# First chunk's rows of the delta rule loaded into other buffers beside the last projections, and the running sum's products issued one column block later

## What is computed

```
proj = x @ w_in                       # qkv, z, beta, a, and more
qkv  = silu(causal_conv(qkv, 4 taps))
q, k = l2norm(q) * 128**-0.5, l2norm(k);  v
beta = sigmoid(beta_logit);  g = -exp(a_log) * softplus(a + dt_bias)
G    = cumsum(g) in a chunk           # the running sum
decay = exp(G_i - G_j), lower triangle
L = strict lower((k*beta) k^T * decay);  T = (I + L)^-1
W = T (k*beta*exp(G));  U = T (v*beta);  A = (q k^T) * decay
per chunk: u = U - W S;  o = (q exp(G)) S + A u;  S = exp(G_last) S + (k exp(G_last - G))^T u
o = o * rsqrt(mean(o*o)) * norm_w * silu(z)
```

## Time and profile before

| what | us |
|---|---|
| median of 3 runs | 3301.83 (3300.44 to 3305.82) |
| the profiled execution | 3304.84 |
| its span (first to last instruction) | 3303.0 |
| PE busy in it | 3039.2 (92%) |
| DVE, ACT, POOL busy | 1425.8, 864.9, 744.4 |

### The profile page before, as it was taken

One profiled execution on the slowest core, in us unless ns is written; L12 is line 12 of the kernel. 1 busy time (PEld: TensorE's weight loads), 2 busy tenths in 40 slices (PEclk: granted clock), 3 DMA queues, 4 the chain that ended last, 5 costly groups with the idle time before them and its releaser, 6 DMA issues.

```text
span 3303.0 us, 36117 instructions
## 1 busy us (share of the span) xinstructions
PE 3039.2 (92%) x15317; PEld 2500.1 (76%) x15317; DVE 1425.8 (43%) x2120; ACT 864.9 (26%) x1225; POOL 744.4 (23%) x481
## 2 busy tenths in 40 slices
PE   8889956589999999999999899799999999999997
PEld 7768745567888888878977899666667878778785
DVE  4776547756333333336244244311135433344335
ACT  3211245431211112222246122211112322222221
POOL 0342301013212212223312355201212111111113
PEclk9989967789999999999999999899999999999998
DMA  4112131221111111111111100211121111111112
GB/s 139 57 53 71 48 94 47 76 96 51 51 46 44 51 52 39 51 51 59 54 39 39 58 14 20 77 38 52 38 89 39 42 48 51 38 51 50 41 51 77
DMA packets 152513, 180.46 MB, mean 55 GB/s; under 512 B 6353, under 2 KB 127889, under 8 KB 152353
## 3 DMA queue, kind: packets, MB, share of 16 engines
q1 hardware_dynamic: 143680, 166.51, 16.2%
q10 hardware_dynamic: 8672, 11.65, 1.0%
HBM read 158.05 MB, written 20.09 MB: 54 GB/s over the span
## 4 chain that ended last, share of the span: by engine, by line
PE 78%; DVE 11%; ACT 3%; POOL 3%; issue 2%; DMA 2%; SPq 0%; ACTq 0%; DVEq 0%; POOLq 0%
PE bank L127 76%; DVE f L158 5%; POOL f L158 3%; DVE f L166 2%; DVE f L175 1%; PE bank L142 1%; ACT f L147 1%; DVE r L158 1%; ACT r L150 1%; DMA f<-gr_s 1%; ACT f L150 1%; DVE f L163 1%; DMA f<-x 0%; DVE f L184 0%; DMA f<-w_in 0%
## 5 line engine op out<-in xcount | busy, mean ns | idle before, releaser
L127 PE MATMUL bank<-r,r 128*128 128x512 f32 (+4 forms) x11592 | 2451.9, 372 | 47.7 <-DVE r L158 25.0
L127 PEld LDWEIGHTS bank<-r,r 128*128 128x128 f32 x11592 | 2020.4, 190 | 470.2 <-issue 51.9
L158 POOL TENSOR_TENSOR f<-f 128x512 f32<-128x512 f32 (+5 forms) x252 | 332.9, 1327 | 1647.1 <-ACT f L147 588.1
L158 DVE TENSOR_TENSOR f<-f,bank 128x512 f32<-128x512 f32 (+2 forms) x519 | 318.5, 635 | 451.3 <-PE bank L127 449.6
L158 DVE TENSOR_TENSOR r<-f,r 128x512 fp32r<-128x512 f32 (+3 forms) x169 | 227.7, 1354 | 507.0 <-ACT r L150 507.0
L127 PE MATMUL bank<-f 128*128 128x128 f32 (+7 forms) x2344 | 329.4, 306 | 74.7 <-DVE f L158 44.0
L150 ACT ACTIVATE r<-f 128x2048 fp32r<-128x2048 f32 (+2 forms) x217 | 278.8, 1308 | 427.0 <-DMA f<-w_up 184.4
L127 PEld LDWEIGHTS bank<-f 128*128 128x128 f32 (+2 forms) x2344 | 282.7, 203 | 106.8 <-issue 44.8
L166 DVE SCALAR_TENSOR_TENSOR f<-f,f 128x1024 f32<-128x1024 f32 (+3 forms) x169 | 202.4, 1205 | 350.5 <-ACT f L147 321.5
L150 ACT ACTIVATE f<-bank 128x512 f32<-128x512 f32 (+8 forms) x340 | 170.5, 509 | 640.7 <-PE bank L127 581.0
L147 ACT ACTIVATE f<-bank 128x512 f32<-128x512 f32 (+1 forms) x175 | 92.0, 527 | 892.7 <-PE bank L127 889.1
(11 more groups left out here) (32 smaller groups left out, 551.8 us busy)
## 6 DMA issues: line engine op xcount, KB each, us to landing
f<-w_in SPq DMA_DIRECT2D x31, 1024.0 KB, 5.4
f<-w_up SPq DMA_DIRECT2D x44, 512.0 KB, 5.2
f<-w_mlp_in SPq DMA_DIRECT2D x16, 1024.0 KB, 5.5
f<-w_mlp_out SPq DMA_DIRECT2D x16, 1024.0 KB, 4.9
f<-w_down SPq DMA_DIRECT2D x11, 1024.0 KB, 5.0
f<-w_out SPq DMA_DIRECT2D x8, 1024.0 KB, 5.2
f<-x_spill SPq DMA_DIRECT2D x4, 2048.0 KB, 11.6
f<-x SPq DMA_DIRECT2D x4, 1024.0 KB, 11.5
```

The source lines that it names most:

```text
L127: return self.g.matmul(out, lhs, rhs, start=start, stop=stop, skip_group_check=True)
L158: return self.g.tensor_tensor(out, a, b, op)
```

## The change

There are two parts.

- **The running sum.** The products "cum", their copies and their exponentials move from block 1 to behind block 2 on PE, ACT and DVE. "rows turned" and its copy move from behind block 2 to behind block 3.
- **Chunk 0's rows.** In set 0 the buffers VB and QG change places with TT and Y of set 1, and these two lie in `k.lnw` (the memory of `S.SQ`), which is free once the last norm is multiplied in (`unit(7)`, in block 9). SP waits for that and for the stored rows, loads chunk 0's rows, and only then waits in `qkv_done`. DVE's diff, ACT's two exponentials, POOL's memset of the state, its mask and its product into QG come ahead of `qkv_done` too. Set 0's E1 and the state lie in neither half of the turned x.

```
+        a, b = self.sets[0], self.sets[1]
+        a[10], a[11], b[5], b[6] = b[5], b[6], a[10], a[11]
...
             ins.then_inc(*k.up("qkv products", "d", "ba rows"))
+        if m == 2:
             b, freed = k.take("d", ALL, "d", "cum")
...
-        if m == 2:
+        if m == 3:
             b, freed = k.take("d", ALL, "d", "rows turned")
...
             g.act(S.an, P["a_log_2"], ACT.Exp).then_inc(*k.up("qkv acts", "d an"))
+        if m == 2:
             g.wait_ge(*k.past("d p", "gc"))
...
-        if m == 2:
+        if m == 3:
             g.wait_ge(*k.past("d", "rows turned"))
...
             then(g.tt(v4(GA), v4(GA), bc(S.an, [128, 8, 4], 1), MUL), "ga")
+        if m == 2:
             g.wait_ge(*k.past("d", "cum"))
...
 def sp_delta(k, g):
     S = k.d
-    qkv_done(k, g)
     g.wait_ge(*k.past("rows stored"))
+    g.wait_ge(*k.past("d", "unit", 7, 1))
     for c in range(NC):
+        if c == 1:
+            qkv_done(k, g)
...
 def act_delta(k, g):
-    qkv_done(k, g)
...
         g.act(E1, E1, ACT.Exp).then_inc(*k.up("delta acts", "d", "e1", c))
+        if c == 0:
+            qkv_done(k, g)
...
 def dve_delta(k, g):
-    qkv_done(k, g)
...
         yield
+        if c == 0:
+            qkv_done(k, g)
         g.wait_ge(*k.past("d", "e1 masked", c))
...
 def pool_delta(k, g):
-    qkv_done(k, g)
...
         g.tt(h4(QG), h4(QG), S.KV[:, 0:4, cs], MUL).then_inc(*k.up(sem, "d", "qg", c))
         yield
+        if c == 0:
+            qkv_done(k, g)
         g.wait_ge(*k.past("d", "LT", c))
```

## The result

| | before | changed |
|---|---|---|
| median of 6 runs each | 3302.93 us (3300.44 to 3313.26) | 3291.74 us (3287.48 to 3295.02) |
| ratio, changed to before | | 0.9957, 95% interval 0.9947 to 0.9967 |
| span of the profiled execution | 3303.0 us | 3285.7 us |

The change makes the kernel faster by 0.43% (0.33 to 0.53%), 14.2 us of 3302.93 by the ratio and 11.2 by the two medians. Measured again, the changed kernel had the ratio 0.9960 (0.9947 to 0.9972). The two profiled spans are 17.3 us apart, more than either figure. Where the 17.3 us lie is read from the same instructions in both traces.

What follows compares the result with a forecast made beforehand. The prediction held that two PE gaps on the path bound what this change could gain. Its terms 7.75 + 5.76 = 13.5 us took the median from 3301.83 to 3288.3 us, range 3284.5 to 3294.5.

Steps and rivals of the forecast that it cites:

- What bounds: Two PE gaps on the path, 5.9 us for DVE and 9.7 for POOL; everything behind moves as a block.
- The running sum, 7.75 us: From "ba rows" to block 4: 34.23 us less 25.84, 0.44 and 0.2, a gain of 7.75 us.
- the upper bound of 0.88: The sum's products on PE: 0.88 us at half clock, bounds 0.3 and 0.88, taken as 0.44.
- the period of 12.92: Undisturbed block with its norm on PE, 12.92 us, counted twice between "ba rows" and block 4.
- The spares: Blocks 2 and 3: 7 us to spare before the sum's products, 6 to 7 before "rows turned".
- ACT's cover of about 1.8 us: Block 2: ACT's work grows to 11.1 us in a period of 12.9, at no cost.
- The rows, 5.76 us: Seam to the delta stage: chunk 0's exponentials end at 1867.40 instead of 1873.16, all 5.76 us reaching PE.
- The landing: Chunk 0's row load behind x's 2 MB load: 7.8 + 4.9 us without overlap, there by 1854.4.
- The clock: Behind the second gap: half clock costs 1.7 us, no gain counted; rival that it holds gives 3286.6 us, chance 0.10.
- the clock would fall at the first gap too: Rival at "ba rows" and block 2: 1.5 to 2.9 us lost, 3289.8 to 3291.2 us, chance 0.07.
- The level: Whole kernel: the median goes from 3301.83 to 3288.3 us.
- The sum of 13.5 us: Whole kernel: 7.75 us from the running sum plus 5.76 us from chunk 0's rows.

Runs made afterwards that it cites:

- the work late: The changed kernel, but ACT, DVE and POOL wait for the projections' end before touching chunk 0; only SP's load is early. Median 3292.36 us, ratio 0.9960.
- the filled gap: The changed kernel with four more 128x512 products on PE, overwritten later, ahead of chunk 0's "t" product. Median 3286.93 us, ratio 0.9946.
- chunk 0 further ahead: The changed kernel with chunk 0's exponentials, mask and first products moved ahead of the last silu and gate. Median 3289.87 us, ratio 0.9948.

## Why the prediction was right

- **What bounds.** Two gaps of PE on the path, everything behind moves as a block. Right as far as it can be seen: the ratio's 14.2 us and the 11.2 of the medians lie on both sides of the 13.9 won at the places, so no loss downstream shows. Behind the delta stage the traces of all kernels spread over 6 us, and a loss of one or two us there would not show.
- **The running sum, 7.75 us.** Measured 7.89. Two terms inside were off and cancelled. The sum's products cost 0.77 us (the group from 1692.88 to 1694.96 is 2.08, a norm alone 1.31), near the upper bound of 0.88 and not the 0.44 taken. And a block that follows small products has its norm 11.29 us after its start (1681.59 to 1692.88), not 11.61 as the one at 1717.52, which began after a norm; so the period of 12.92 was too long for block 2. The same 0.35 us shows in block 4, which lasts 12.57 us behind "rows turned". That the total is right to 0.14 us is luck in this respect.
- **The spares.** DVE copied the sums by 1700.15 and PE came to "rows turned" at 1707.87; expected were 6 to 7 us between them, there were 7.7. ACT's copy of block 3's second half waited 2.70 us for PE, so ACT's cover of about 1.8 us held.
- **The rows, 5.76 us.** Measured 5.67. ACT became the end of this chain as told. The landing was overestimated: 7.8 + 4.9 = 12.7 us without overlap, measured 8.1 from issue to DVE's start. Two things were off. The 4.9 was the median of three row loads in a queue, and chunk 0's own had landed in 3.8. And the two loads overlapped: x's own took 7.9 us from an issue 0.5 us earlier, and DVE started 0.7 us after it had landed. It changed nothing in the sum, since ACT came to the rows 15 us later.
- **The clock.** It fell in the gap of 4.07 us as in the one of 9.73, so no gain was right for the sum. The argument behind it was weak: it set the new gap's 4.0 us against the 3.6 to 4.1 after which the clock had fallen before, and here the clock fell 2.1 to 2.3 us after the last product, and with the work late more than 4.9 us after it. The price was taken as 1.7 us. Against the filled gap it is 1.69 in the kernel before (5.62 less 3.93) and 2.09 in the changed one, which thus paid 0.4 more. That the clock would fall at the first gap too did not happen (1.00 from 1681.70 on).
- **The level.** 3288.3 was told and the median is 3291.74. The sum of 13.5 us lies between the 11.2 of the medians and the 14.2 of the ratio, and the two places show 13.56 (13.9 with block 4). Of the 3.4 us from 3288.3 to the median, 1.1 are the kernel before, whose median went from 3301.83 with three runs to 3302.93 with six, and 2.3 are what the difference of the medians lacks to 13.5. Neither place of the change shows a loss of that size, so I take them for spread. In the profiled executions "ba rows" begins anywhere from 1678.44 to 1685.47 (1681.00 in the changed kernel, 1682.63 before), ahead of anything that differs between these kernels. A median of three runs is no better known than that.

## What to carry to other kernels

A barrier that guards memory holds work that doesn't touch the memory. Find for each engine which buffer it truly waits for, and give the first step of the next stage a buffer that comes free earlier; the load's latency (here 3.8 us) and the wait for the gate with the first vector work (1.9) then leave the path one by one. The table load stayed on it behind the last silu; it left it (1.3 us) only where ACT waited for something else, or where the exponentials were placed ahead of the last silus. A short product that waits for a chain of small operations belongs behind the next large block of the in-order engine, and what is won there is the wait and the clock that the wait would have cost (5.9 and about 2 us). When gains are a few us in 3300, judge them between landmarks on both sides of the edit, since the spans here differed by 3.4 us for reasons outside it, and two traces of one kernel by 5.8.

## What was not expected of the hardware

Work thrown away can be worth its time: 3.60 us of products into a bank that is overwritten kept the granted clock at 1.00 and brought the next level 2.09 us earlier, although nothing used their result. A gap of 2.15 us kept the clock (one trace), and gaps of 4.07 us and more lost it in all seven traces that had one. The length of the gap does not settle it, though: in a gap of 4.07 us the clock fell 2.1 to 2.3 us after the last product, and in one of 5.97 us it was still at 1.00 after 4.9, so it is not shown that a gap of 2.15 us would keep it every time. And DVE's product of LT with the beta rows, 128x512, took 1.01 us with the work late, 0.81 in the changed kernel and 0.69 in the version with chunk 0 further ahead. POOL's product of the same size still ran beside its first 0.47, 0.26 and 0 us; that this is the cause was not tested.
